# Opening of a two-layer transformer kernel: value projection on x times the norm weight, deviation applied later, ones multiplied on TensorE in the waits

## The chip, the core and the metric

The kernel runs on one core of a Trainium2 chip. The metric is the device time of one execution in microseconds (us), as the median of several runs. The core has a matrix engine (TensorE, PE in the rows; its weight loads are PEld), a vector engine (VectorE, DVE), an activation engine (ScalarE, ACT), GpSimd (POOL, almost unused here) and SyncE (SP), which issues all of the transfers of this kernel from one queue. All numbers of the kernel are float32; before a projection, the activations and the weights are each split into a rounded part (hi) and a rest (lo), and each product is taken as three matmuls, hi by hi, hi by lo and lo by hi.

## What is computed

A gated mixing block, then two transformer layers (differential attention and latent attention, each with a gated convolution feed-forward part), for 256 tokens of width 1024. The change lies in the first microseconds of the first block alone:

```
h = rmsnorm(x, norm_mix_g)            # x / sqrt(mean(x*x) + eps) * g, row by row
proj = h @ w_in                       # 1024 x 7168; split into u, v, bg, cg, xs, ga, gb
u = gelu(u)
v = rmsnorm(gelu(v), norm_v_g)
a = spatial_gating(u, v, w_s, b_s)    # u * (masked w_s @ v + b_s), 8 groups
c = bg * causal_dwconv(cg * xs, conv_w)
m = sigmoid(ga) * (a @ w_proj_a) + sigmoid(gb) * (c @ w_proj_b)
x = x + m @ w_out
...
```

The deviation of a row of x is one factor for the whole row, so v before its gelu is ((x * g) @ w_v) times that factor, and the factor can be applied to the product.

## The kernel before, in words

The program writes the order of each engine out by hand, with semaphores between the engines. Weights come in chunks n = 0, 1, 2, ...: a transfer into a landing buffer (raw, and for chunks 2 and 3 raw_start), ACT writes the hi part into a ring of four slots (whl), DVE the lo part, PE multiplies, and a chunk's slot is free once PE has used it (chunk_used). Chunks 0 to 3 (N_V) are the value projection; each is half of the 1024 rows of the weight by 512 columns. They come in two transfers each (half_landed, rest_landed) and are split in two halves (split_hi_half on ACT, line 1243; split_lo_half on DVE, line 1769), which count half_lo and lo_ready. Chunks 4 to 19 (N_MIX) are four passes over the columns of cg, xs, bg and u; they are loaded by load_mix (line 477 for the first two, line 443 after that), which waits until the landing buffer is free (lo_ready), and split as a whole (lines 1221 and 1707).

The opening, by engine:

- SP issues x_rows[0] (line 459), the identity matrix (460), norm_mix_g (461), x_rows[1] (462), and then the eight half chunks (467, 468).
- DVE sets constants (1786 to 1791), among them the zeros of wsT (1790). const_set counts them.
- PE turns norm_mix_g into columns (684), and DVE copies it to mix_g (1793). PE transposes x_rows of the first 128 tokens (turn_x, line 690) for the residual.
- ACT squares and sums the rows of x as they land (1275) and takes the root (1277); DVE takes the reciprocal (1796) and scales the rows into vtok (1797). PE transposes the scaled rows of both token blocks, and then x_rows of the second block.
- ACT rounds the transposed rows times mix_g to hT (round_h, 1248), DVE writes the rest (rest_h, 1775), with the two halves of chunk 0 among them. h_ready counts the finished tiles.
- PE's v_rows (710 to 725) multiplies chunk by chunk: stationary a tile of hT, moving 512 columns of the weight; 2 token blocks x 4 k-tiles x 3 matmuls a chunk (lines 616 to 618), 96 in all. ACT applies gelu (take_v, 1294) into vtok.
- The mixer then calls project (609 to 611) for chunks 4, 5, 6, 7. Ahead of chunk 5 PE turns the small vectors (turn_vectors), ahead of chunk 6 the rows of w_s (turn_ws, line 744), and ahead of chunk 7 it runs the spatial mixing (mix_tokens, line 766, 32 matmuls), which waits for v_norm, for ws_read (DVE's four copies in take_ws, lines 1827 and 1828) and for vec_read.
- DVE copies the transposed x out of PSUM to xT (1808); it is needed in the first block's end.

## Time and profile before

| | before |
|---|---|
| median of 3 runs | 1051.89 us (1051.37 to 1051.95) |
| the profiled execution, its own time | 1052.46 us |
| its span | 1050.7 us |
| PE busy | 1028.6 us |
| DVE busy | 729.9 us |
| ACT busy | 572.0 us |
| mean DMA rate over the span | 170 GB/s |

The page gives busy time by engine over the whole span, and the chain of work that ended last. For a change in the opening the timeline and the windows of the first 60 us are the views to read: a stretch of the timeline lists instructions in order of time, one line for a merged group, with its start, its duration, its engine and source line, what it writes and reads, its count, and in brackets the engine's idle time just before it and what ended it.

### The profile page before, as it was taken

What the parts mean: (1) busy time and instruction counts of PE and PEld (TensorE: products, weight loads), DVE (VectorE), ACT (ScalarE), POOL (GpSimd) and SP (SyncE); (2) the same over time, 40 slices, a digit from 0 to 9 for tenths busy, and PEclk for the clock granted to TensorE, in tenths of its full rate; (3) what the DMA queues carried; (4) which work ended last, traced back from release to release, by engine and by line L of the source; (5) the groups of instructions that cost most, each with busy time, mean ns of one, the idle gap of its engine ahead of it and who ended that gap; (6) DMA issues with size and microseconds to landing.
All of it is one profiled execution on the core that took longest, in us unless ns stands there. A gap on an engine that the chain in (4) does not pass through costs nothing.

```text
span 1050.7 us, 19999 instructions
## 1 busy us (share of the span) xinstructions
PE 1028.6 (98%) x7892; PEld 990.1 (94%) x7892; DVE 729.9 (69%) x969; ACT 572.0 (54%) x795; POOL 6.6 (1%) x20
## 2 busy tenths in 40 slices
PE   7999999999999999999999999999999989999997
PEld 6999999999999999978899999999989989999996
DVE  6676654558665456777878777777876577777775
ACT  6555566545443443567866555554637464555554
POOL 0000000000000000000000000000020000000000
PEclk9999999999999999999999999999999999999999
DMA  8636565455655644453555666663434374666651
GB/s 292 205 124 197 180 200 196 160 182 179 214 187 196 203 160 166 158 198 121 168 153 159 203 180 180 180 180 111 136 71 120 113 212 139 190 189 189 188 159 75
DMA packets 191266, 178.89 MB, mean 170 GB/s; under 512 B 17444, under 2 KB 169586, under 8 KB 191218
## 3 DMA queue, kind: packets, MB, share of 16 engines
q1 hardware_dynamic: 191218, 178.22, 54.6%
q8 instruction: 34, 0.56, 0.2%
q14 instruction: 14, 0.11, 0.0%
HBM read 177.15 MB, written 1.05 MB: 170 GB/s over the span
## 4 chain that ended last, share of the span: by engine, by line
PE 89%; DVE 5%; ACT 3%; DMA 2%; issue 1%; SPq 0%; DVEq 0%; ACTq 0%
PE psum L609 24%; PE psum L611 24%; PE psum L610 24%; PE psum L616 4%; PE psum L617 4%; PE psum L618 4%; DVE whl L1707 2%; ACT whl L1221 1%; PE psum L950 1%; PE psum L934 1%; PE psum L949 1%; ACT prob L1462 1%; DMA x_rows<-x 1%; DMA raw<-da_w_qkv 0%; DVE stat L2084 0%
## 5 line engine op out<-in xcount | busy, mean ns | idle before, releaser
L609 PE MATMUL psum<-hT,whl 128*128 128x256 f32 x1392 | 395.9, 284 | 4.3 <-DVE hT L1782 4.3
L611 PE MATMUL psum<-hT,whl 128*128 128x256 f32 x1392 | 394.4, 283 | 0.0
L610 PE MATMUL psum<-hT,whl 128*128 128x256 f32 x1392 | 394.3, 283 | 0.0
L1707 DVE TENSOR_TENSOR whl<-raw,whl 128x2048 fp32r<-128x2048 f32 (+2 forms) x145 | 298.3, 2063 | 92.1 <-ACT whl L1221 91.8
L1221 ACT ACTIVATE whl<-raw 128x2048 fp32r<-128x2048 f32 (+2 forms) x145 | 248.7, 1717 | 113.0 <-DMA raw<-w_ff 67.9
L609 PEld LDWEIGHTS psum<-hT,whl 128*128 128x128 f32 x1392 | 267.3, 192 | 6.0 <-DVE hT L1782 4.2
L610 PEld LDWEIGHTS psum<-hT,whl 128*128 128x128 f32 x1392 | 267.3, 192 | 0.9
L611 PEld LDWEIGHTS psum<-hT,whl 128*128 128x128 f32 x1392 | 267.3, 192 | 0.0
L609 PE MATMUL psum<-lat,whl 128*128 128x256 f32 (+1 forms) x512 | 145.8, 285 | 0.0
L610 PE MATMUL psum<-lat,whl 128*128 128x256 f32 (+1 forms) x512 | 144.7, 283 | 0.0
L611 PE MATMUL psum<-lat,whl 128*128 128x256 f32 (+1 forms) x512 | 144.7, 283 | 0.0
L1393 ACT ACTIVATE conv_out<-conv_in,vcol 128x256 f32<-128x256 f32 x88 | 48.2, 595 | 122.7 <-DVE conv_in L1983 122.7
L609 PEld LDWEIGHTS psum<-lat,whl 128*128 128x128 f32 (+1 forms) x512 | 97.2, 190 | 0.4 <-DVE k_sb L2243 0.3
L610 PEld LDWEIGHTS psum<-lat,whl 128*128 128x128 f32 (+1 forms) x512 | 97.2, 190 | 0.1
L611 PEld LDWEIGHTS psum<-lat,whl 128*128 128x128 f32 (+1 forms) x512 | 97.2, 190 | 0.0
L1981 DVE SCALAR_TENSOR_TENSOR conv_out<-conv_in,vcol,conv_out 128x256 f32<-128x256 f32 x176 | 73.6, 481 | 8.9 <-ACT conv_out L1393 8.1
L1707 DVE TENSOR_TENSOR whl<-q_sb,whl 128x2048 fp32r<-128x2048 f32 (+1 forms) x44 | 77.1, 1751 | 1.6 <-ACT whl L1221 1.6
L1983 DVE TENSOR_TENSOR conv_in<-psum,rstd 128x512 f32<-128x512 f32 x44 | 30.4, 691 | 53.2 <-PE psum L611 53.1
L1221 ACT ACTIVATE whl<-q_sb 128x2048 fp32r<-128x2048 f32 (+1 forms) x44 | 65.0, 1478 | 2.5 <-PE psum L611 2.5
L609 PE MATMUL psum<-mT,whl 128*128 128x256 f32 x192 | 54.7, 285 | 0.8 <-DVE mT L2121 0.8
L610 PE MATMUL psum<-mT,whl 128*128 128x256 f32 x192 | 53.9, 281 | 0.0
L611 PE MATMUL psum<-mT,whl 128*128 128x256 f32 x192 | 53.9, 281 | 0.0
(246 smaller groups left out, 1386.7 us busy)
## 6 DMA issues: line engine op xcount, KB each, us to landing
raw<-w_ff SPq DMA_DIRECT2D x32, 1024.0 KB, 5.5
raw<-w_in SPq DMA_DIRECT2D x24, 1024.0 KB, 5.2
raw<-ffn_w_up SPq DMA_DIRECT2D x44, 512.0 KB, 5.0
q_sb<-ffn_w_up SPq DMA_DIRECT2D x44, 512.0 KB, 5.0
raw<-da_w_qkv SPq DMA_DIRECT2D x12, 1024.0 KB, 5.2
q_sb<-ffn_w_down SPq DMA_DIRECT2D x22, 512.0 KB, 3.6
raw<-ffn_w_down SPq DMA_DIRECT2D x22, 512.0 KB, 3.6
raw<-w_proj_a SPq DMA_DIRECT2D x4, 1024.0 KB, 5.2
```

The costliest lines, as they stand in the source:

```text
L609: mm(dst, weight(n, 0, cols, kt, c0, m), hi, start=start, stop=False, skip_group_check=True)
L610: mm(dst, weight(n, 0, cols, kt, c0, m), lo, start=False, stop=False, skip_group_check=True)
L611: return mm(dst, weight(n, 1, cols, kt, c0, m), hi, start=False, stop=stop, skip_group_check=True)
L616: mm(dst, hi, w_hi, start=start, stop=False, skip_group_check=True)
L617: mm(dst, hi, w_lo, start=False, stop=False, skip_group_check=True)
L618: return mm(dst, lo, w_hi, start=False, stop=stop, skip_group_check=True)
L934: last = nc.tensor.transpose(pxs[:, c, s * P:(s + 1) * P], weights[:, c, s * P:(s + 1) * P], ident)
L1221: fn(whl[:, slot, 0, 0:w], landing(n)[:, 0:w], ACT.Copy).then_inc(hi_ready, 1)
L1393: ins = fn(conv_out[:, q, b, :], conv_in[:, q, b, 2:], ACT.Identity, bias=conv(3, b, j), scale=conv(2, b, j))
L1707: tt(whl[:, slot, 1, 0:w], landing(n)[:, 0:w], whl[:, slot, 0, 0:w].bitcast(F32), ALU.subtract).then_inc(lo_ready, 1)
L1981: return stt(dst, conv_in[:, q, b, t:SEQ + t], vcol[:, bass.ds(j + (conv_col(l - 1, t) + FB * b), 1)], dst, ALU.mult, ALU.add)
L1983: tt(conv_in[:, q, :, 2:], up[q][:], scale, ALU.mult).then_inc(f["up_read"], 1)
```

## The change

In the opening, the value projection no longer reads the normalised rows. It reads u = x times norm_mix_g, in transposed tiles of 128 x 128, held in the buffers lat (k-tiles 0 to 3) and mT (k-tiles 4 to 7), which are otherwise used later (opening, round_u, rest_u). The reciprocal deviation of the row is given to the gelu as its scale (take_v). The sums of squares, the root, the scaling of the rows (now in place in x_rows) and their transposes move behind: ACT does them after the splits of chunks 0 to 2, DVE after those splits too, and PE transposes the scaled rows between the chunks 2 and 3 of the value projection (turn_rows_of_h). round_h and rest_h, which now serve the chunks from 4 on alone, come after the gelu of the first half of v and around the splits of chunks 4 and 5; project for chunk 4 waits for their tiles one by one.

PE multiplies a 128 x 128 matrix of equal numbers by itself (busy) 10 times at the very start, 12 times between the two blocks of transposes of x, and 8 times after them. All of x is transposed before the value projection. Chunk 0 is taken in another order: k-tiles 0 and 1 of both token blocks, then 2 and 3 of both.

On SP's queue, x_rows[1] goes behind the first half of chunk 0, and the transfer of b_s waits until PE has used chunks 0 to 3. The zeros of wsT move from DVE's start to take_ws.

The diff, cut to its edits:

```diff
--- before.py
+++ after.py
@@ -342,6 +342,7 @@
...
         x_turned, x_read = sem("x_turned"), sem("x_read")
+        u_hi_ready, u_ready = sem("u_hi_ready"), sem("u_ready")
         vec_turned, vec_read = sem("vec_turned"), sem("vec_read")
...
@@ -387,6 +388,11 @@
...
+        def opening(kt):
+            return (lat if kt < KT // 2 else mT)[:, kt, :, :]
...
@@ -459,12 +465,13 @@
...
             sp.dma_start(vec_rows[0:KT, 0, :], a["norm_mix_g"].rearrange("l (r c) -> (l r) c", c=P)).then_inc(mix_landed, 16)
-            sp.dma_start(x_rows[:, 1, :], x_in[:, 1, :]).then_inc(x_landed[1], 16)
             for n in range(N_MIX):
...
                 sp.dma_start(dst[:, 0:KT // 4, :], src[:, 0:KT // 4, :]).then_inc(half_landed[n], 16)
+                if n == 0:
+                    sp.dma_start(x_rows[:, 1, :], x_in[:, 1, :]).then_inc(x_landed[1], 16)
                 sp.dma_start(dst[:, KT // 4:, :], src[:, KT // 4:, :]).then_inc(rest_landed[n], 16)
...
@@ -502,6 +509,8 @@
...
+            sp.wait_ge(chunk_used, N_MIX)
             sp.dma_start(bsb[:], a["b_s"].broadcast_to([P, A_GROUPS, P])).then_inc(bsb_landed, 16)
...
@@ -654,10 +663,6 @@
...
-            def h_tile(k):
-                return lambda kt: pe.wait_ge(h_ready, KT * k + kt + 1)
...
@@ -679,28 +684,47 @@
...
+            def busy(count):
+                for _ in range(count):
+                    mm(bank[2][:, 0, 0:P], ones[D][:], ones[D][:], start=True, stop=True)
+            pe.wait_ge(const_set, 2)
+            busy(10)
             pe.wait_ge(ident_landed, 16)
...
-            def turn_x(dst, src, t, done):
+            pe.wait_ge(mix_g_read, 1)
+            for t in range(TT):
+                if t > 0:
+                    busy(12)
+                pe.wait_ge(x_landed[t], 16)
                 for kt in range(KT):
-                    last = nc.tensor.transpose(dst[kt // 2][:, kt % 2, t * P:(t + 1) * P],
-                                               src[:, t, kt * P:(kt + 1) * P], ident)
-                    if done is not None and kt % 2 == 1:
-                        last.then_inc(done, 1)
-            pe.wait_ge(x_landed[0], 16)
-            turn_x(x_bank, x_rows, 0, None)
-            pe.wait_ge(mix_g_read, 1)
-            pe.wait_ge(xn_ready, 1)
-            turn_x(bank, vtok, 0, None)
-            pe.wait_ge(xn_ready, 2)
-            turn_x(bank, vtok, 1, xn_turned)
-            pe.wait_ge(x_landed[1], 16)
-            turn_x(x_bank, x_rows, 1, x_turned)
+                    last = nc.tensor.transpose(x_bank[2 * t + kt // 4][:, kt % 4 // 2, kt % 2 * P:(kt % 2 + 1) * P],
+                                               x_rows[:, t, kt * P:(kt + 1) * P], ident)
+                    if kt % 4 == 3:
+                        last.then_inc(x_turned, 1)
+            busy(8)
+            def turn_rows_of_h():
+                pe.wait_ge(x_read, 4)
+                for t in range(TT):
+                    pe.wait_ge(xn_ready, t + 1)
+                    for kt in range(KT):
+                        last = nc.tensor.transpose(x_bank[kt // 2][:, kt % 2, t * P:(t + 1) * P],
+                                                   x_rows[:, t, kt * P:(kt + 1) * P], ident)
+                        if t == TT - 1 and kt % 2 == 1:
+                            last.then_inc(xn_turned, 1)
+            def h_tile(k):
+                return lambda kt: pe.wait_ge(h_ready, KT * k + kt + 1)
...
@@ -710,22 +734,27 @@
                 order = [(t, at) for t in range(TT) for at in range(KT // 2)]
+                if n == 0:
+                    order.sort(key=lambda o: o[1] // 2)
                 for t, at in order:
...
                         pe.wait_ge(lo_ready, n + 1)
-                    if t == 0 and n < 2:
-                        pe.wait_ge(h_ready, max(2, kt + 1))
+                    if n < 2:
+                        pe.wait_ge(u_ready, KT * t + kt + 1)
                     w_hi, w_lo = [weight(n, part, 2 * PAIR, at, 0, 2 * PAIR) for part in range(2)]
-                    last = tokens(flat(bank[n // 2 * 2 + t]), n, w_hi, w_lo, hi_lo(hT, kt), t, kt == 0, kt == KT - 1)
+                    last = tokens(flat(bank[n // 2 * 2 + t]), n, w_hi, w_lo, (opening(kt)[:, 0, :], opening(kt)[:, 1, :]), t, kt == 0,
+                                  kt == KT - 1)
                     if t == 0 and kt == KT - 1:
...
                 v_rows(N_V + c)
+                if c == 2:
+                    turn_rows_of_h()
...
@@ -754,7 +783,8 @@
...
                         mix_tokens()
-                    project(N_MIX + s, hT, i)
+                    first = s == 0 and spatial
+                    project(N_MIX + s, hT, i, first=h_tile(MIX) if first else None)
...
@@ -877,7 +907,6 @@
...
-            pe.wait_ge(const_set, 2)
             pe.wait_ge(const_landed, 16)
...
@@ -1242,10 +1271,17 @@
...
+            def round_u(t, kts):
+                for kt in kts:
+                    act.wait_ge(x_turned, 2 * t + kt // 4 + 1)
+                    fn(opening(kt)[:, 0, t * P:(t + 1) * P], x_bank[2 * t + kt // 4][:, kt % 4 // 2, kt % 2 * P:(kt % 2 + 1) * P],
+                       ACT.Identity, scale=mix_g[:, kt:kt + 1]).then_inc(u_hi_ready, 1)
...
                 act.wait_ge(xn_turned, kt // 2 + 1)
-                fn(hT[:, kt, 0, :], bank[kt // 2][:, kt % 2, :], ACT.Identity, scale=mix_g[:, kt:kt + 1]).then_inc(h_hi, 1)
+                fn(hT[:, kt, 0, :], x_bank[kt // 2][:, kt % 2, :], ACT.Identity, scale=mix_g[:, kt:kt + 1]).then_inc(h_hi, 1)
...
@@ -1265,25 +1301,29 @@
...
+            x_bank = [up[0], up[1], px, py]
+            half = KT // 2
             act.wait_ge(const_set, 1)
-            fn(eps[:, 1:2], eps[:, 0:1], ACT.Sqrt)
+            fn(eps[:, 1:2], eps[:, 0:1], ACT.Identity)
+            act.wait_ge(mix_g_read, 1)
+            round_u(0, range(0, half))
+            split_hi_half(0, 0)
+            round_u(0, range(half, KT))
+            round_u(1, range(0, half))
+            split_hi_half(0, 1)
+            round_u(1, range(half, KT))
+            for n in (1, 2):
+                split_hi_half(n, 0)
+                split_hi_half(n, 1)
             x_flat = t_act[:].rearrange("p a b c -> p (a b c)")
             for t in range(TT):
-                act.wait_ge(x_landed[t], 16)
                 if t > 0:
...
                 fn(x_flat, x_rows[:, t, :], ACT.Square, accum_out=xstat[:, 0, t:t + 1]).then_inc(x_sq, 1)
-                act.wait_ge(x_sq, t + 1)
-                fn(xstat[:, 1, t:t + 1], xstat[:, 0, t:t + 1], ACT.Sqrt, bias=eps[:, 0:1], scale=1.0 / D).then_inc(x_std, 1)
-            split_hi_half(0, 0)
-            act.wait_ge(mix_g_read, 1)
-            for kt in range(KT):
-                if kt == KT // 2:
-                    split_hi_half(0, 1)
-                round_h(kt)
-            split_hi_half(1, 0)
-            split_hi_half(1, 1)
+            act.wait_ge(x_sq, TT)
+            fn(xstat[:, 1, :], xstat[:, 0, :], ACT.Sqrt, bias=eps[:, 0:1], scale=1.0 / D).then_inc(x_std, 1)
+            split_hi_half(3, 0)
+            split_hi_half(3, 1)
...
@@ -1292,18 +1332,15 @@
...
                 fn(vtok[:, t, 2 * g * PAIR:2 * (g + 1) * PAIR], bank[2 * g + t][:].rearrange("p a b -> p (a b)"),
-                   ACT.Gelu).then_inc(bank_free[2 * g + t], 1)
-            for c in range(4):
-                n = N_V + c
-                if n + LEAD < N_MIX:
-                    split_hi_half(n + LEAD, 0)
-                    split_hi_half(n + LEAD, 1)
-                else:
-                    split_hi(n + LEAD)
-                if c == 1:
-                    for t in range(TT):
-                        take_v(0, t)
+                   ACT.Gelu, scale=xstat[:, 2, t:t + 1]).then_inc(bank_free[2 * g + t], 1)
+            act.wait_ge(xn_ready, 1)
+            take_v(0, 0)
+            take_v(0, 1)
+            split_hi(N_MIX)
+            for kt in range(KT):
+                round_h(kt)
+            split_hi(N_MIX + 1)
             t_flat = t_act[:].rearrange("p a b c -> p (a b c)")
...
@@ -1772,7 +1809,7 @@
...
                 dve.wait_ge(h_hi, kt // 2 * 2 + 2)
-                stt(hT[:, kt, 1, :], bank[kt // 2][:, kt % 2, :], mix_g[:, kt:kt + 1], hT[:, kt, 0, :].bitcast(F32),
+                stt(hT[:, kt, 1, :], x_bank[kt // 2][:, kt % 2, :], mix_g[:, kt:kt + 1], hT[:, kt, 0, :].bitcast(F32),
                     ALU.mult, ALU.subtract).then_inc(h_ready, 1)
...
@@ -1787,25 +1824,42 @@
...
                 nc.vector.memset(ones[w][:], 1.0 / w)
-            nc.vector.memset(wsT[CHUNK:P, :, 0:CHUNK], 0.0)
             nc.vector.memset(conv_in[:, :, :, 0:2], 0.0).then_inc(const_set, 1)
...
             copy(mix_g[:], bank[3][:, 0, 0:KT]).then_inc(mix_g_read, 1)
-            for t in range(TT):
-                dve.wait_ge(x_std, t + 1)
-                step.wait(step.mark(nc.vector.reciprocal(xstat[:, 2, t:t + 1], xstat[:, 1, t:t + 1])))
-                ts(vtok[:, t, :], x_rows[:, t, :], xstat[:, 2, t:t + 1], None, ALU.mult).then_inc(xn_ready, 1)
+            x_bank = [up[0], up[1], px, py]
+            def rest_u(t, kts):
+                for kt in kts:
+                    dve.wait_ge(u_hi_ready, KT * t + kt // 4 * 4 + 4)
+                    stt(opening(kt)[:, 1, t * P:(t + 1) * P], x_bank[2 * t + kt // 4][:, kt % 4 // 2, kt % 2 * P:(kt % 2 + 1) * P],
+                        mix_g[:, kt:kt + 1], opening(kt)[:, 0, t * P:(t + 1) * P].bitcast(F32), ALU.mult,
+                        ALU.subtract).then_inc(u_ready, 1)
+            half = KT // 2
+            dve.wait_ge(mix_g_read, 1)
+            rest_u(0, range(0, half))
             split_lo_half(0, 0)
-            dve.wait_ge(mix_g_read, 1)
-            for kt in range(KT):
-                if kt == KT // 2:
-                    split_lo_half(0, 1)
-                rest_h(kt)
+            rest_u(0, range(half, KT))
+            rest_u(1, range(0, half))
+            split_lo_half(0, 1)
+            rest_u(1, range(half, KT))
             split_lo_half(1, 0)
             split_lo_half(1, 1)
-            for b, src in enumerate((up[0], up[1], px, py)):
-                dve.wait_ge(x_turned, b + 1)
-                copy(xT[:, 2 * b:2 * b + 2, :], src[:]).then_inc(x_read, 1)
+            for t in range(TT):
+                for b in range(2):
+                    copy(xT[:, 4 * b:4 * b + 4, t * P:(t + 1) * P],
+                         x_bank[2 * t + b].rearrange("p a (b c) -> p (a b) c", c=P)).then_inc(x_read, 1)
+            split_lo_half(2, 0)
+            split_lo_half(2, 1)
+            dve.wait_ge(x_std, 1)
+            step.wait(step.mark(nc.vector.reciprocal(xstat[:, 2, :], xstat[:, 1, :])))
+            dve.wait_ge(x_turned, 4)
+            for t in range(TT):
+                ts(x_rows[:, t, :], x_rows[:, t, :], xstat[:, 2, t:t + 1], None, ALU.mult).then_inc(xn_ready, 1)
+            split_lo_half(3, 0)
+            split_lo_half(3, 1)
...
@@ -1821,6 +1875,7 @@
...
+                nc.vector.memset(wsT[CHUNK:P, :, 0:CHUNK], 0.0)
                 for u in range(2):
...
@@ -1839,13 +1894,10 @@
...
-            for c in range(4):
-                n = N_V + c + LEAD
-                if n < N_MIX:
-                    split_lo_half(n, 0)
-                    split_lo_half(n, 1)
-                else:
-                    split_lo(n)
+            split_lo(N_MIX)
+            for kt in range(KT):
+                rest_h(kt)
+            split_lo(N_MIX + 1)
             dve.wait_ge(v_std, 1)
...
             for t in range(TT):
```

## Rows read from the trace of the kernel before

**Rows 1.** The page, part 1 and part 4: busy engines, and the chain.

```profile
PE 1028.6 (98%) x7892; PEld 990.1 (94%) x7892; DVE 729.9 (69%) x969; ACT 572.0 (54%) x795; POOL 6.6 (1%) x20
...
PE 89%; DVE 5%; ACT 3%; DMA 2%; issue 1%; SPq 0%; DVEq 0%; ACTq 0%
```

**Rows 2.** Busy time by stretch, core's first 50 us; header line names the columns.

```profile
core 0: us, PE busy (x) PEld busy (x) DVE busy (x) ACT busy (x) POOL busy (x), PEclk, DMA share, GB/s
0.00:10.00 10.00, 4.08 (x17) 3.31 (x17) 2.91 (x12) 5.18 (x9) 0.20 (x4) 1.00 0.77 265
10.00:20.00 10.00, 9.77 (x43) 8.69 (x44) 9.42 (x16) 9.12 (x16) 0.00 (x0) 1.00 1.03 370
...
40.00:50.00 10.00, 10.00 (x88) 10.00 (x87) 8.62 (x14) 4.21 (x4) 0.00 (x0) 1.00 0.55 181
```

**Rows 3.** Timeline of PE, first 14.6 us and where chunk 4 begins.

```profile
4.56 0.24 PE L684 MATMUL psum<-const,vec_rows 8*128 8x8 f32 x1 [4.56 <-DMA vec_rows<-norm_mix_g]
4.73 1.97 PE L690 MATMUL psum<-const,x_rows 128*128 128x128 f32 x8
6.76 1.94 PE L690 MATMUL psum<-const,vtok 128*128 128x128 f32 x8
10.23 1.97 PE L690 MATMUL psum<-const,vtok 128*128 128x128 f32 x8 [1.53 <-DVE vtok L1797]
11.99 1.92 PE L690 MATMUL psum<-const,x_rows 128*128 128x128 f32 x8
13.56 0.67 PE L616 MATMUL psum<-whl,hT 128*128 128x512 f32 x1
...
14.07 0.40 PE L617 MATMUL psum<-whl,hT 128*128 128x512 f32 x1
...
14.30 0.40 PE L618 MATMUL psum<-whl,hT 128*128 128x512 f32 x1
...
35.65 0.28 PE L609 MATMUL psum<-hT,whl 128*128 128x256 f32 x1
```

**Rows 4.** The chain in order of time, later small matmuls: start, duration, line, count.

```profile
47.75 0.88 PE psum L744 x8
...
54.38 3.57 PE psum L766 x32
```

**Rows 5.** Timeline of DVE and ACT, first 24 us.

```profile
1.50 0.48 DVE L1790 MEMSET wsT<- 64x512 f32 x1
4.83 0.17 DVE L1793 COPY mix_g<-psum 128x8 f32<-128x8 f32 x1 [2.74 <-PE psum L684]
7.72 1.06 ACT L1275 ACTIVATE t_act<-x_rows 128x1024 f32<-128x1024 f32 x1 [2.09 <-DMA x_rows<-x]
9.42 0.75 DVE L1797 TENSOR_SCALAR vtok<-x_rows,xstat 128x1024 f32<-128x1024 f32 x1
16.74 3.95 ACT L1243 ACTIVATE whl<-raw_start 128x1024 fp32r<-128x1024 f32 x4
18.55 2.48 DVE L1808 COPY xT<-psum 128x512 f32<-128x512 f32 x4
20.71 1.28 ACT L1294 ACT_TABLE_LOAD   x1
20.94 4.62 DVE L1769 TENSOR_TENSOR whl<-raw_start,whl 128x1024 fp32r<-128x1024 f32 x4
```

**Rows 6.** Transfers: first half of chunk 0 (issued 2.46), then its rest (2.93).

```profile
raw<-w_in SPq DMA_DIRECT2D x1, 512.0 KB, 6.5
...
raw<-w_in SPq DMA_DIRECT2D x1, 512.0 KB, 7.4
```

**Rows 7.** Groups by line and shape: busy, mean ns of one, idle before.

```profile
L1486 ACT ACTIVATE t_act<-hf 128x128 f32<-128x128 f32 x16 | 4.7, 302 | 0.9 <-DVE hf L2108 0.9
L1775 DVE SCALAR_TENSOR_TENSOR hT<-psum,mix_g,hT 128x256 fp32r<-128x256 f32 x8 | 3.3, 476 | 0.6 <-ACT hT L1248 0.6
```

**Rows 8.** Timeline of DVE and ACT, 25 to 54 us, and PEld at mix_tokens.

```profile
39.32 0.17 DVE L1850 RECIPROCAL vstat<-vstat 128x2 f32<-128x2 f32 x1 [7.42 <-ACT vstat L1316]
...
47.79 0.69 DVE L1887 TENSOR_TENSOR conv_in<-psum,t_act 128x512 f32<-128x512 f32 x1 [0.36 <-PE psum L611]
...
49.30 1.92 ACT L1221 ACTIVATE whl<-raw 128x2048 fp32r<-128x2048 f32 x1 [5.29 <-DMA raw<-w_in]
...
53.27 0.43 DVE L1828 COPY wsT<-psum 64x256 f32<-64x256 f32 x1
...
54.10 3.66 PEld L766 LDWEIGHTS psum<-wsT,vtok 128*128 128x128 f32 x32
54.22 3.73 PE L766 MATMUL psum<-wsT,vtok 128*128 128x128 f32 x32
```

## The prediction

> **What bounds the kernel now.** I began with the page: TensorE is busy 1028.6 of 1050.7 us, and 89% of the chain that ended last is its own [rows 1]. Then the windows of the opening: in the first 10 us TensorE works 4.08 us, in the next ten 9.77, later all of it [rows 2]. So the idle time that a change of the opening can give back lies before 10.2 us. Then TensorE's timeline: it waits for the transfers until 4.56, works through the first transposes, waits 1.53 us (1.9 with its weight loads) for the scaled rows of the second token block, and runs without a gap from 10.23 [rows 3]. The chain behind that wait is plain in the other engines' rows: x_rows[1] lands at 7.7, is squared, scaled from 9.42 on, transposed [rows 5]. Last, the spacing of instructions shows a second loss. Eight transposes take 1.97 us with the 0.42 us of the last one's own duration in it, so one comes every 0.22 us [rows 3]; eight of the same kind at 47.75 take 0.88, 0.11 each [rows 4]. The granted clock reads 1.00 in all windows [rows 2] and does not show it, but the spacing is that of 1.2 GHz early and of 2.4 GHz late. The first matmul of 512 columns starts at 13.56, the second at 14.07 (0.51 us, low clock), the third at 14.30 (0.23, high clock) [rows 3]: the clock rose at about 14.
>
> From 13.56 the 96 matmuls of the value projection take 96 x 0.227 = 21.8 us plus 0.28 for the first, and chunk 4 starts at 35.65 [rows 3]. From there TensorE is never idle for long, so the whole is a matter of when the work behind the opening begins. I sum everything as a shift of that start, and add it to the end.
>
> **The change part by part.** *TensorE's work.* It transposes 32 tiles before and 32 after; what moves is that the 16 of the scaled rows now stand between chunks 2 and 3 at the high clock, on the path: 16 x 0.11 = 1.76 us [rows 4]. If the value projection begins at S, chunk 4 begins at S + 21.8 + 1.8 = S + 23.5, a shift of S - 12.1 against 35.65. The change gains only if S is below 12.1.
>
> *The ones.* A product of 128 x 128 by 128 columns costs 3.57 / 32 = 0.11 us at the high clock [rows 4] and 0.22 at the low one, as the transposes do [rows 3]. Ten from about 1.6 (the zeros of wsT, 0.48 us [rows 5], no longer stand before the count they wait for) end at 3.8, before the row of norm_mix_g is there at 4.56: free. TensorE now waits for the copy of mix_g, which ends at 5.00 [rows 5], so the first block of x is transposed from 5.05 instead of 4.73 to 6.8. Twelve ones: to 9.5 at the low clock.
>
> *x_rows[1] behind the first half of chunk 0.* Before, the one landed at 7.7 [rows 5], the other at 2.46 + 6.5 = 9.0, the rest of chunk 0 at 10.3 [rows 6]. Both are 512 KB, so I let them change places: the weights at 7.8, x at 9.0; bounds for x 8.3 and 10.3. It is thus about there when the twelve ones end.
>
> *Clock.* All low: transposes 9.5 to 11.3, eight ones to 13.0, so S = 13.0. All high from 8.9 on: x is awaited to 9.0, transposes to 9.9, ones to 10.8, S = 10.8. Before, the clock rose after 3.8 us of unbroken work from 10.23; but the 4 us from 4.56, with a gap of 0.4 us in the weight loads, didn't raise it [rows 3]. After, the work is unbroken from 5.05 while x is in time, so I expect the rise between 8.9 and 12.4; at 10.3, the middle, S = 11.6. That is my value.
>
> The Trainium skill speaks against this in "TensorE: Matmul & The Clock Gate", Part 4: transposes are said not to count as work that lets the clock rise. By that rule only the ones would count, and it is the first rival below. In this trace 16 transposes and half a microsecond of matmuls stood before the rise, which speaks against the rule.
>
> *ACT and DVE.* They must deliver as fast. A rounding of a 128 x 128 tile on ACT takes 302 ns by the nearest row, a rest on DVE less than the 476 ns of a 128 x 256 one [rows 7]; back to back I take 0.27 and 0.26. ACT: first four tiles 6.2 to 7.3, first half of chunk 0 7.8 to 8.8, four tiles to 9.9, four of the second block (transposed by 10.5) to 11.6, second half of chunk 0 to 12.6. DVE follows: first half's lo at 10.2, below S; second half's lo at 13.9. TensorE wants it at S + 12 x 0.227 = 14.3, since chunk 0 now begins with tiles 0 and 1 of both blocks. No stall at S = 11.6; at S = 10.8 one of up to 0.4. Chunk 1 is ready at 17.5 (wanted 18.4). The copies to xT, 2.48 us, and the halves of chunk 2 at 1.15 each [rows 5] end at 22.3 (wanted 23.9). Squares, a table load of 1.28 [rows 5], and root end on ACT at 22, the scaled rows on DVE at 23.6; TensorE wants them at 27.9. Chunk 4's lo is there at 30.2 and the last tile of h at 33.5, for a start at 35.1. The margins are over one microsecond, so these parts cost nothing; if they all came 1.6 us later, the excess would go to the path.
>
> *Queues.* load_mix of chunk 7 waits for chunk 5's lo, now about 36.7, and lands at about 42.6; chunk 7 is wanted at 54. The wait before b_s stands behind it in the queue, ends at 35, and b_s is read at 57. ACT waits 5.29 us for chunk 8 as it is [rows 8]. Free.
>
> *The zeros of wsT.* 0.48 us plus a gap, 0.52, now stand in DVE's row from 47.79, which waits for TensorE (0.36 us idle) and therefore moves with it, to the last copy of take_ws, over at 53.70. TensorE's weight load at 54.10 waits for that copy [rows 8]: slack 0.34 with the signal, so 0.52 costs 0.18 us, on the path.
>
> *Sum:* 11.6 - 12.1 + 0.18 = -0.35 us. Bounds: S = 10.8 with its stall -0.8, all high and the zeros hidden -1.3; S = 13.0 gives +1.1. The profiled execution took 1052.46 with a span of 1050.7; it would take 1052.1. It stands 0.6 above the median of 1051.89, which the same shift brings to 1051.5.
>
> **The rivals.** *The clock stays low until the projection has run for a while (slower).* Place: twelve and eight ones with eight transposes between them, if transposes and the small matmuls don't suffice, or a wait for x breaks the work. S = 13.0, and the matmuls of chunk 0 pay 0.2 us each until the rise: at 14 the total is +1.1 + 0.4 + 0.2 = +1.6, 1053.5, still in the band of no change; if the rise waits for 3.8 us of projection, to 17, ten matmuls pay and the stalls of chunk 0 lie under them: +2.9, 1054.8. It becomes slower than 0.2% from a rise at about 15. For it: 4 us of transposes at 4.56 didn't raise the clock. Against: the 3.8 us from 10.23 did.
>
> *x lands late.* Behind four transfers instead of three; if it comes at 12 the transposes end at 13 to 14, ACT's rounding of the second block holds chunk 0 and the total is about +2.5, 1054.4. Against: the landings before are 1.3 us apart [rows 6].
>
> *The chain is shorter than I take it.* If the first half of chunk 0 lands at 7.0, x at 8.0 and the clock is high by then, S is 9.8 and the lo of the second half comes at 12.4: -2.3 + 0.2, 1049.8. It needs three things at once.
>
> *The change does nothing it says:* the ones neither raise the clock nor does S move below 12.1; that is the first rival's milder half.
>
> **How the numbers follow.** About 0.2%, 2.1 us, is what a measurement of this kernel can tell from no change. My forecast, S from 10.8 to 12.7, 1050.6 to 1052.7: 0.72. Low clock till 14, 1053.5: 0.12. Low clock till 17, 1054.8: 0.05. Late x, 1054.4: 0.04. Shorter chain, 1049.8: 0.07. So faster 0.07, same 0.84, slower 0.09. The range leaves out the last three in the main and reaches from 1050.2 to 1053.6.
>
> **What would show it.** In the profile after: first transposes at 5.05; x_rows[1] landed at 9.0; the spacing of the eight transposes of block two and of the ones after them, 0.22 turning to 0.11; first matmul of 512 columns at 11.6; 16 transposes at about 28 that take 1.8 us; project of chunk 4 from 35.1 without a wait for h_ready; a short wait of TensorE for wsT's last copy at 54. Wrong if the first matmul of 512 columns starts below 10 or above 14, or if chunk 4 waits for DVE.

## The result, and the profile after

| | before | changed |
|---|---|---|
| median | 1051.92 us (6 runs, 1051.33 to 1053.64) | 1056.07 us (6 runs, 1054.13 to 1056.97) |
| ratio to before, 95% interval | | 1.0036 (1.0024 to 1.0048) |
| the profiled execution, its own time | 1052.46 us | 1056.26 us |
| its span | 1050.7 us | 1054.5 us |

The change makes the kernel slower by 4.1 us between the medians, 0.36% by the ratio. The forecast was 1051.5, no change, with a range to 1053.6; the result lies outside it.

The page of the changed kernel, parts 1 and 4, answers to [rows 1]:

```profile
PE 1034.7 (98%) x7952; PEld 996.2 (94%) x7952; DVE 734.0 (70%) x984; ACT 577.2 (55%) x811; POOL 6.6 (1%) x20
...
PE 89%; DVE 5%; ACT 3%; DMA 1%; issue 1%; DVEq 0%; ACTq 0%
```

TensorE executes 60 matmuls more. The program has 30 products of ones. So each product is two matmuls, which the prediction had not counted. TensorE's timeline of the changed kernel, the opening, answers to [rows 3]:

```profile
1.42 4.64 PE L691 MATMUL psum<-ones 128*128 128x128 f32 x20 [1.42 <-DVE conv_in L1827]
5.98 0.27 PE L697 MATMUL psum<-const,vec_rows 8*128 8x8 f32 x1
6.51 1.54 PE L707 MATMUL psum<-const,x_rows 128*128 128x128 f32 x8 [0.26 <-DVE mix_g L1829]
7.89 2.84 PE L691 MATMUL psum<-ones 128*128 128x128 f32 x24
10.57 1.04 PE L707 MATMUL psum<-const,x_rows 128*128 128x128 f32 x8
11.45 1.95 PE L691 MATMUL psum<-ones 128*128 128x128 f32 x16
13.15 0.48 PE L625 MATMUL psum<-whl,lat 128*128 128x512 f32 x1
...
37.10 0.28 PE L618 MATMUL psum<-hT,whl 128*128 128x256 f32 x1
```

The chain of work that ended last (start, duration, line, count) runs in the same execution, from 1.42 to 13.4 us, through the ones and the transposes:

```profile
1.42 4.64 PE psum L691 x20
6.51 1.54 PE psum L707 x8
8.05 2.68 PE psum L691 x24
10.74 0.87 PE psum L707 x8
11.61 1.79 PE psum L691 x16
```

The first row of ones lasts to 6.0, past the 4.56 at which norm_mix_g had been there [rows 3]. The clock rises in the first transposes of x (eight in 1.54 us, then eight in 1.04), some 6 us earlier than in the kernel before. What follows at the high clock is mostly the multiplying of ones: 2.68 and 1.79 us in the chain. The value projection starts at 13.15, against 13.56, and chunk 4 at 37.10, against 35.65: a shift of 1.45 us.

The shift grows twice more. I set the n-th matmul of one trace, counted from the end, against the n-th of the other. The shift is 1.45 us at chunk 4, 2.1 to 2.2 from the spatial mixing on, 2.0 up to 507 us, and 3.8 from 513 to the end. The timeline of ACT, DVE and TensorE up to the spatial mixing, changed kernel, answers to [rows 8]:

```profile
44.05 1.92 ACT L1250 ACTIVATE whl<-raw 128x2048 fp32r<-128x2048 f32 x1 [0.39 <-DMA raw<-w_in]
...
46.00 2.29 DVE L1744 TENSOR_TENSOR whl<-raw,whl 128x2048 fp32r<-128x2048 f32 x1 [0.75 <-ACT whl L1250]
...
49.71 0.69 DVE L1939 TENSOR_TENSOR conv_in<-psum,t_act 128x512 f32<-128x512 f32 x1 [0.32 <-issue]
...
53.43 0.48 DVE L1878 MEMSET wsT<- 64x512 f32 x1 [0.17 <-DVE conv_out L1928]
...
55.81 0.43 DVE L1883 COPY wsT<-psum 64x256 f32<-64x256 f32 x1
...
56.34 3.81 PE L796 MATMUL psum<-wsT,vtok 128*128 128x128 f32 x32 [0.51 <-issue]
```

TensorE waits 0.51 us for the last copy of take_ws, which ends at 56.24; the view calls it "issue", since it names no releaser. The second growth is at the load of the attention's output weight. The waits of 495 to 516 us (who waited for whom, total, times, longest) in the kernel before:

```profile
ACT whl L1221 <- DMA raw<-da_w_o: 1.2, 1, 1.2
```

and in the changed kernel:

```profile
ACT whl L1250 <- DMA raw<-da_w_o: 2.9, 1, 2.9
...
PE psum L978 <- ACT k_sb L1568: 1.2, 1, 1.2
```

### The profile page after: what moved, and what is told of

It is laid out like the page before. It is cut to its first block, busy times and chain, and to the rows that moved or that the text cites. A ratio compares the mean times of both kernels' runs of the same rounds, so it can differ in the third digit from the quotient of the medians.

```text
span 1054.5 us, 20151 instructions
## 1 busy us (share of the span) xinstructions
PE 1034.7 (98%) x7952; PEld 996.2 (94%) x7952; DVE 734.0 (70%) x984; ACT 577.2 (55%) x811; POOL 6.6 (1%) x20
## 4 chain that ended last, share of the span: by engine, by line
PE 89%; DVE 5%; ACT 3%; DMA 1%; issue 1%; DVEq 0%; ACTq 0%
PE psum L618 24%; PE psum L619 24%; PE psum L620 24%; PE psum L625 4%; PE psum L626 4%; PE psum L627 4%; DVE whl L1744 2%; ACT whl L1250 1%; PE psum L691 1%; PE psum L979 1%; DMA raw<-da_w_o 1%; PE psum L963 1%; PE psum L978 1%; ACT prob L1499 1%; DVE stat L2136 0%
## 5 line engine op out<-in xcount | busy, mean ns | idle before, releaser
L2035 DVE TENSOR_TENSOR conv_in<-psum,rstd 128x512 f32<-128x512 f32 x44 | 30.4, 691 | 53.2 <-PE psum L620 53.1
```

The source lines that it names most:

```text
L2035: tt(conv_in[:, q, :, 2:], up[q][:], scale, ALU.mult).then_inc(f["up_read"], 1)
```

## The experiments

Each time is a median beside the median of the kernel before measured with it, which lies between 1051.9 and 1052.2. Where one is set against the changed kernel, it is against 1056.07.

**Half of the ones.** `busy(5)`, `busy(6)`, `busy(4)` for 10, 12, 8:

```diff
-            busy(10)
+            busy(5)
-                    busy(12)
+                    busy(6)
-            busy(8)
+            busy(4)
```

> The changed kernel with 5, 6 and 4 products of ones instead of 10, 12 and 8; nothing else. Theory (a product of ones is two weight loads and two matmuls, so it costs 0.43 us at the low and 0.22 us at the high clock, twice what the prediction took): the first row of ones is over at 3.6 instead of 6.1, norm_mix_g is turned at 4.56 instead of 5.98, the value projection starts between 10.8 and 12.5 instead of 13.15, most likely 11.7, and the kernel is 1.4 us faster than the changed one, about 1054.6 against 1056.1. Rival (the loss comes from elsewhere, the ones only fill waits): the value projection starts within 0.3 us of 13.15 and the time is within 0.5 us of the changed kernel's. Second rival (fewer ones, later rise of the clock): the start is early but matmuls of 512 columns take 0.43 us each until 14, and half of the gain is gone.

Measured: 1053.40 us against 1051.90, ratio 1.0009 (1.0001 to 1.0018), so 2.7 us less than the changed kernel. TensorE's timeline of the opening:

```profile
1.42 2.50 PE L691 MATMUL psum<-ones 128*128 128x128 f32 x10 [1.42 <-DVE conv_in L1827]
4.58 0.24 PE L697 MATMUL psum<-const,vec_rows 8*128 8x8 f32 x1 [0.66 <-DMA vec_rows<-norm_mix_g]
5.08 1.97 PE L707 MATMUL psum<-const,x_rows 128*128 128x128 f32 x8 [0.26 <-DVE mix_g L1829]
6.84 2.77 PE L691 MATMUL psum<-ones 128*128 128x128 f32 x12
9.40 1.92 PE L707 MATMUL psum<-const,x_rows 128*128 128x128 f32 x8
11.11 1.10 PE L691 MATMUL psum<-ones 128*128 128x128 f32 x8
11.97 0.48 PE L625 MATMUL psum<-whl,lat 128*128 128x512 f32 x1
```

This is the opening that the prediction described, line by line: transposes from 5.08 (5.05), ones to 9.4 (9.5), the clock's rise in the last row of ones, the projection at 11.97 (11.6). The double price of the ones is shown. Chunk 4 starts at 35.9, a shift of 0.25, so 1.2 us earlier than in the changed kernel, and the mixing 1.7 us earlier. The median fell by 2.7, twice the 1.4 that were expected; the opening does not account for all of it, and the profiled execution, at 1056.26 us, was the slowest of the twelve.

**No ones.** All three calls of busy taken out.

> The changed kernel without any product of ones. Theory (the ones cost more on the path than the higher clock gives back): transposes from 5.05 at 0.22 us each, x_rows[1] awaited to 8.9, value projection from 10.7 at the low clock, 0.43 us a matmul, until the clock rises; if it rises at 14, chunk 4 starts 0.8 us earlier than in the changed kernel, about 1055.3; if it rises at 12, 1.8 us earlier, 1054.3. Rival (the clock is what the opening lives on): the clock rises only at 17 or later and the kernel is slower than the changed one, 1057 or more.

Measured: 1052.93 us against 1051.90, ratio 1.0008 (0.9999 to 1.0017). TensorE's timeline:

```profile
5.02 1.97 PE L704 MATMUL psum<-const,x_rows 128*128 128x128 f32 x8 [0.26 <-DVE mix_g L1825]
9.38 1.97 PE L704 MATMUL psum<-const,x_rows 128*128 128x128 f32 x8 [2.38 <-DMA x_rows<-x]
11.00 0.78 PE L625 MATMUL psum<-whl,lat 128*128 128x512 f32 x1
11.57 0.63 PE L626 MATMUL psum<-whl,lat 128*128 128x512 f32 x1
12.00 0.63 PE L627 MATMUL psum<-whl,lat 128*128 128x512 f32 x1
```

The first matmuls of 512 columns come at the low clock, one every 0.43 us (the first takes 0.57), and the clock rises at about 14. The kernel still is 3.1 us faster than the changed one. So the clock is worth something: each of six matmuls cost 0.20 us more, 1.2 us in all. The 30 products spent more than that. Chunk 4 starts at 36.27, 0.8 us earlier than in the changed kernel, just as expected for a rise at 14. The time, however, is 2.4 us below the 1055.3 expected with it, so here too the median fell by more than the opening shows.

**u in another buffer.** k-tiles 4 to 7 of u in a buffer at hf's address; in return the zeros of wsT are set on DVE at the start, and b_s is loaded without its wait.

```diff
-            return (lat if kt < KT // 2 else mT)[:, kt, :, :]
+            if kt < KT // 2:
+                return lat[:, kt, :, :]
+            return u_more[:, kt - KT // 2, :, :]
...
-            sp.wait_ge(chunk_used, N_MIX)
...
-                nc.vector.memset(wsT[CHUNK:P, :, 0:CHUNK], 0.0)
```

> The changed kernel with k-tiles 4 to 7 of u in a buffer at hf's address instead of mT; since mT lies over wsT and bsb, the zeros of wsT can then be set on DVE at the start again and b_s loaded without the wait for chunk 3; both are done here. Theory 1 (the zeros in take_ws hold the spatial mixing): TensorE's wait of 0.51 us ahead of mix_tokens is gone and the kernel is 0.5 us faster than the changed one. Theory 2 (matmuls whose stationary tile is read from mT's address are slower, 0.233 against 0.227 us): with hf they take 0.227, another 0.3 us, 1055.3 in all. Rival for 2 (the spacing belongs to chunks 1 and 3, not to the buffer): 0.233 stays, gain 0.5 us at most.

Measured: 1054.36 us against 1051.90, ratio 1.0026 (1.0016 to 1.0037), 1.7 us less than the changed kernel. Three rows of TensorE's timeline of the changed kernel, chunk 3, whose stationary tiles come from mT:

```profile
35.24 0.40 PE L626 MATMUL psum<-whl,mT 128*128 128x512 f32 x1
35.47 0.39 PE L627 MATMUL psum<-whl,mT 128*128 128x512 f32 x1
35.70 0.40 PE L625 MATMUL psum<-whl,mT 128*128 128x512 f32 x1
```

There the mean spacing is 0.2333 us in chunks 1 and 3, in each of five profiles that read mT, against 0.2267 in chunk 2, which reads lat. With the other buffer chunk 1 is back at 0.2267 and chunk 3 at 0.2285, with its slower ones right behind the transposes. So 48 matmuls cost 48 x 0.0066 = 0.3 us through the buffer alone. What a buffer's address has to do with the spacing is not shown. At the mixing, DVE's last copy ends at 54.88 and TensorE starts without a wait:

```profile
55.40 1.83 PE L800 MATMUL psum<-wsT,vtok 128*128 128x128 f32 x15
```

The distance from chunk 4 to the mixing is 18.57 us, that of the kernel before, instead of 19.24. In the trace both theories hold: chunk 4 comes 0.26 us and the mixing 0.94 us earlier than in the changed kernel. The median fell by 1.7 us instead of the 0.8 expected, but 1 us lies within what two series of these kernels can differ by, as the kernel before once more shows below.

**The changed kernel once more.**

> The changed kernel unchanged, as a second profile. In the first one the shift against the kernel before is 1.45 us where chunk 4 starts, 2.13 after the spatial mixing, and 3.79 at the end; 1.6 us came in between 507 and 516, where the transfer of da_w_o landed late. Theory (the 1.6 us are chance of that execution and its transfers): this profile has the first two shifts within 0.3 us, and the wait at 508 differs, by up to 2 us in either direction, so the time of single executions spreads by that much. Rival (the shifted opening makes the later transfer late): the wait for da_w_o is 2.9 us again and the end is shifted by 3.8 again.

Measured: 1055.93 us against 1051.90, ratio 1.0037 (1.0025 to 1.0050). In this profile the clock was high from 5.9 us, before the first transposes of x (eight in 1.09 us), the projection started at 12.64, and chunk 4 was shifted by 0.9 us, the mixing by 1.5. So the opening itself spreads by half a microsecond from one execution to the next, and the expected 0.3 us were too few. ACT's wait for da_w_o was 1.9 us: less than 2.9, more than the 1.2 of the kernel before. The end is shifted by 2.0 us, not 3.8, so the rival does not hold as put, but the late transfer is there again.

**Small products in the kernel before.** 8 products of 8 x 8 ahead of the wait for the identity, 7 between the transposes of the scaled blocks.

```diff
+            def small(count):
+                for _ in range(count):
+                    mm(px[0:8, 1, P:P + 8], ones[D][:, 0:8], ones[D][:, 0:8], start=True, stop=True)
...
+            small(8)
...
             turn_x(bank, vtok, 0, None)
+            small(7)
```

> The kernel before with 15 products of 8 x 8 on TensorE in its idle time (8 ahead of the wait for the identity, 7 between the transposes of the two scaled blocks): as many instructions, 60, as the ones of ones_half, and nothing on the path. Theory (the instructions added shift the blocks in which TensorE's instructions are fetched; in the kernels with ones a fetch falls at 500 to 502 us, into the transfer of da_w_o, which then lands late, in the two profiles without ones it falls at 508 to 509): the fetch is at about 500 here too, TensorE or ACT wait 0.5 to 2 us longer around 508, and the time is 0.7 to 1.5 us above the kernel before although the opening is the same within 0.2 us. Rival (chance): same time as the kernel before within 0.4 us. The clock may rise earlier through the small products, worth up to 1.5 us the other way; the trace shows it.

Measured: 1051.84 us against 1052.23, ratio 0.9998 (0.9989 to 1.0006). The 16 KB fetch moved from 508 to 498 us as expected, and nothing came of it: ACT waited 1.1 us. The theory as put fell. What remained was that the 8 KB fetch had stayed at 506.3.

The opening wasn't the same, though. In this profile the clock rose at 10.4 us instead of 13 to 14, and it brought little:

```profile
8.74 0.51 PE L684 MATMUL psum<-ones 128*8 128x8 f32 x14
9.18 1.65 PE L696 MATMUL psum<-const,vtok 128*128 128x128 f32 x8
10.67 1.04 PE L696 MATMUL psum<-const,x_rows 128*128 128x128 f32 x8
11.95 0.47 PE L616 MATMUL psum<-whl,hT 128*128 128x512 f32 x1 [0.24 <-DVE hT L1782]
```

TensorE now waits for hT, and later for the second half of chunk 0. Chunk 4 starts at 34.3, 0.2 us before it does in the two profiles below that have this opening without the small products.

**The zeros of wsT alone, in the kernel before.** The memset of line 1790 moved into take_ws.

> The kernel before with the zeros of wsT set in take_ws, as the change does, and nothing else. Theory (DVE's row up to the last copy of take_ws holds mix_tokens): the copy ends at 54.2 instead of 53.7, the 32 small matmuls begin 0.2 to 0.6 us later and the whole is 0.2 to 0.6 us longer, 1052.3. The prediction took 0.18, the changed kernel showed 0.67 between chunk 4 and the mixing. Rival: it costs nothing, same as before within 0.1 in the trace at 54 us.

Measured: 1052.25 us against 1052.23. In the trace, the mixing starts 18.77 us after chunk 4 instead of 18.57, so 0.20 us are lost. That is the prediction's 0.18, and below what the total time tells.

**The kernel before once more.**

> The kernel before, unchanged, as a second profile. The opening should agree within 0.3 us, up to the point where the clock rises (theory: the rise isn't tied to the program, so the first matmul of 512 columns may come at either clock); the fetch of instructions near 508 us should recur within 1 us and ACT's wait for da_w_o should be 0.9 to 1.5 us. Rival (chance in the transfers): a wait for da_w_o of 2 us or more in this profile too.

Measured: 1051.20 us against 1052.23. TensorE's timeline:

```profile
8.97 1.97 PE L690 MATMUL psum<-const,vtok 128*128 128x128 f32 x8 [0.36 <-DVE vtok L1797]
10.73 1.92 PE L690 MATMUL psum<-const,x_rows 128*128 128x128 f32 x8
12.30 0.78 PE L616 MATMUL psum<-whl,hT 128*128 128x512 f32 x1
```

The opening did not agree within 0.3 us. x_rows[1] landed at 6.4 us instead of 7.7, so the second block of scaled rows came 1.3 us earlier than in [rows 3], and chunk 4 at 34.5 instead of 35.65. In before_small and before_zeros, whose openings are nearly the same, x_rows[1] landed at 6.2 and 6.6 and chunk 4 starts at 34.3 and 34.6. The one profile that the prediction rested on was the latest of four, by 1.1 us. The fetches (506.6 and 507.1 us) and ACT's wait (1.3 us) were as expected.

The time says something too. This is the same kernel as the one beside it, and its median of nine executions lies 1.0 us lower (ratio 0.9993, 0.9984 to 1.0002). So a difference of 1 us between two medians of this document can be chance.

**Other buffer and six ones.** u_in_hf with `busy(6)` between the blocks of transposes, and no other ones.

> The changed kernel with u's k-tiles 4 to 7 at hf's address (and zeros and b_s as in the kernel before), and of the ones only 6 products, between the two blocks of transposes. Theory (what remains of the change when the ones are priced rightly and the buffer is another): norm_mix_g turned at 4.55, transposes from 5.05 to 6.8, ones to 9.4, transposes to 11.1, value projection from 11.0, with some matmuls at 0.43 us until the clock rises between 10 and 13; chunk 4 starts between 35.0 and 35.9, mixing within 0.5 us of the kernel before; 24 instructions more than before. Time 1051.5, if the fetch of instructions doesn't fall into da_w_o's transfer; 1052.5 if it does.

Measured: 1050.82 us against 1052.23, ratio 0.9991 (0.9982 to 1.0000). The opening came earlier than expected: the clock rose at 8.7, not after 10, the projection started at 9.80 and chunk 4 at 34.1, below the 35.0 to 35.9 that were expected. **The same again:**

> hf_0_6_0 unchanged, once more, against the kernel before. Theory (its opening is worth about 0.6 us, chunk 4 at 34.2 to 35 against 34.3 to 35.7, and no pair of fetches meets da_w_o's transfer): median 0.5 to 1.5 us below the kernel before's, ratio 0.9990. Rival (the first measurement was luck): within 0.3 us of the kernel before.

Measured: 1050.82 us against 1052.09, ratio 0.9992 (0.9984 to 1.0001). The two medians lie 1.4 and 1.3 us below those of the kernel before. Each interval reaches 1, and the kernel before once more lay 1.0 us below itself, so a small gain is likely and not shown. In the traces chunk 4 starts at 34.1 and 33.9, 0.2 to 0.7 us before the three profiles above. TensorE's timeline of the second:

```profile
4.93 1.97 PE L710 MATMUL psum<-const,x_rows 128*128 128x128 f32 x8 [0.26 <-DVE mix_g L1832]
6.69 2.31 PE L695 MATMUL psum<-ones 128*128 128x128 f32 x12
8.84 1.04 PE L710 MATMUL psum<-const,x_rows 128*128 128x128 f32 x8
9.71 0.49 PE L629 MATMUL psum<-whl,lat 128*128 128x512 f32 x1
```

x_rows[1] landed at 8.1 us and the ones end 0.7 us later. The clock rose among them, and the projection starts at 9.71 at the high clock. At 12.96 TensorE waits 0.23 us for the second half of chunk 0, so an earlier start would have gained little. Why the clock rose at 8.4 and 8.7 here, and at 11.2 in ones_half with the same six products in this gap and five more ahead of them, is open.

**Five, twelve, eight.** The changed kernel with the first row of ones halved.

> The changed kernel with 5 products of ones at the start instead of 10. Theory (the first row's second half, past 4.56, is pure loss): norm_mix_g is turned at 4.57 instead of 5.98 and the value projection starts 1.4 us earlier than the changed kernel's if the clock rises as early, about 11.9, with the second row costing 5.1 at the low clock or 2.7 at the high one. Median 1055 against 1056, between the changed kernel and ones_half. Rival (the first row is what raises the clock at 6 to 8 us; with 5 it rises at 10 or later): the second row then takes 4 us or more, and the value projection starts at 13 or later, no gain against the changed kernel.

Measured: 1056.60 us against 1052.09, ratio 1.0038 (1.0023 to 1.0053): no gain.

```profile
6.73 4.05 PE L691 MATMUL psum<-ones 128*128 128x128 f32 x24
```

The rival forecast the times rightly: the second row (24 matmuls) took 4.05 us, not 2.84, and the projection started at 13.20. The clock rose at 9.3 instead of 7.5. That the shorter first row is what delayed it is not shown, since in hf_again, with no first row at all, it rose at 8.4. Here the load of chunk 7 landed at 44.9 (44.0 in the changed kernel), DVE waited 1.58 us for ACT's part of it (0.75), and TensorE 1.3 us at the mixing.

**Both fetches together, the opening good.** hf_0_6_0 with 9 small products in the first idle time.

> hf_0_6_0 with 9 products of 8 x 8 in TensorE's idle time before the identity lands: 60 instructions more than the kernel before instead of 24, opening otherwise the same. In the profiles so far, da_w_o's transfer landed late (ACT waited 1.9 to 3.5 us, TensorE 0.2 to 1.8 us for k_sb) in those four where two fetches of instructions, of 16 KB and of 8 KB, both began within 0.4 us of 500 us (counted in the kernel before's time), and on time (0.9 to 1.3 us) in the six where only one did or none. Theory (the pair delays it): here the 16 KB one moves to the 8 KB one, ACT waits 2 us or more, and the median is 0.7 to 1.5 us above hf_0_6_0's 1050.8. Rival (the late landing is chance or belongs to something else of the change): median within 0.4 us of 1050.8, wait about 1.

Measured: 1051.32 us against 1052.09, ratio 0.9996 (0.9987 to 1.0005), 0.5 us above hf_0_6_0. The queues of instructions between 498 and 500.5 us in this kernel (packets, MB, share) show that both fetches fell there:

```profile
q8 instruction: 1, 0.02, 2.6%
q14 instruction: 1, 0.01, 1.1%
```

In hf_again the same question for 496 to 500 us gives one of them, and the other follows at 503:

```profile
q14 instruction: 1, 0.01, 0.8%
```

ACT waited 1.6 us (1.0 in hf_0_6_0 and hf_again). The expected wait of 2 us or more and the 0.7 us in the median were not reached. The wait points the way of the theory, but is shorter than in any of the profiles that it was made from; 0.5 us in the median can be chance.

## Why the prediction was wrong, point by point

**The ones: the step that failed.** The prediction read 3.57 us for x32 at line 766 [rows 4] and took 32 for the number of products. The code issues 8 groups by 2 blocks there, 16 products. Each float32 product is two matmuls with two weight loads (20 in the first row's line for ten calls), unlike a transpose, which is one (8 for eight). A product of ones costs 0.22 us at the high and 0.43 at the low clock. So the ten took 4.64 us and not 2.2, put norm_mix_g off from 4.56 to 5.98, and the second and third row took 4.5 us of the chain at the high clock, where 20 products at the prediction's 0.11 come to 2.2. The projection started at 13.15 instead of 11.6. The kernel with half of them started it at 11.97, within the bounds of 10.8 and 12.7, and 1.2 us before the changed one.

This step alone would have left the result in the range: with S at 13.15 the prediction's own sum gives +1.2 us, 1053.1. The measured shift is 4.1 us against a sum of -0.35. Besides the 1.55 us of S, it took the path up to chunk 4 (0.4), the load of chunk 7 (0.5), the late profile the sum was set against (1.1) and the load at 500 us (0.8 and 1.7 in the two profiles). Halving the ones took 2.7 us of the 4.1 away and leaving them out 3.1, more than the 1.7 and 1.3 us by which the mixing came earlier in the two traces. The remainder lies behind the opening, or is chance.

**The clock.** Its rise was looked for between 8.9 and 12.4; it came at 5.9 and 7.5 in the two profiles of the changed kernel, at the end of the first row of ones and in the first transposes, and at 11.2 in ones_half, inside. The value of 10.3 was called the middle of the bounds, which is 10.65; that moves S by less than 0.2. The first rival (low clock to 14 or 17) didn't come to pass; in ones_none it rose at 14 and cost 1.2 us. The Trainium skill's rule in "TensorE: Matmul & The Clock Gate", Part 4, that transposes don't let the clock rise, isn't decided: in both profiles of the kernel before it rose after transposes and at most two projection matmuls (at 14.0 and 12.9), which speaks against it. In the kernels with ones it rose after ones, and in ones_none it rose at 13.8, after six projection matmuls, which fits it.

**The path between.** S + 23.5 was to give chunk 4. With S = 13.15 that is 36.7, and it came at 37.1. The 0.3 us of mT's slower spacing were put at nothing in the sum; the 16 transposes took 1.75 us in the chain (1.76 forecast). Right were also: x_rows[1] at 8.9 (2.51 + 6.4; 9.0 forecast), the first half of chunk 0 at 7.5 (7.8), and the margins of ACT and DVE up to chunk 4: TensorE waited for none of them.

**The zeros of wsT.** 0.18 forecast, 0.20 alone in the kernel before. But the changed kernel lost 0.67 there. "Free" was said of chunk 7, whose load now waits for a later lo of chunk 5: it was issued at 38.2 (36.7 forecast) and landed at 44.0 (42.6 forecast), ACT waited 0.39 us for it, and its split on DVE started at 46.00, after a wait of 0.75 us (0.62 before). Measured from chunk 4, that split ends 0.5 us later than in the kernel before, and it pushed the whole row of DVE up to take_ws. I had looked at when TensorE wants chunk 7 (54 us) and not at what stands behind its split on DVE. Nor had I seen why the zeros move at all: mT lies over wsT and bsb, so the choice of buffer forces both the memset and the wait of b_s.

**The load at 500 us** stood in no rival. The changed kernel's median lies 4.1 us above; its opening explains about 2.6, the distance of the means at the mixing (56.3 and 55.7, against 54.2, 53.1, 52.9 and 53.3 in the four profiles with the opening of before). Of the rest, 1.5 us, its two profiles show 1.7 and 0.8 coming in between 507 and 513. There ACT waited for da_w_o 1.9 to 3.5 us in five profiles, and 0.9 to 1.6 in the other eight. The 3.5 us are those of ones_half's slowest execution. In those five, and in hf_small with 1.6, a 16 KB and an 8 KB fetch of instructions began within 0.5 us of each other near 500 us, while that transfer was under way. In the seven others at most one of them fell there; in the kernel before both come at 508, when the chunk has landed at 504.6. So instructions added at the start move fetches that come hundreds of microseconds later. That the pair causes the late landing is not shown. It fits all thirteen profiles, but hf_small made the pair and ACT waited only 0.6 us longer than in hf_again, and whether something else of the changed opening takes part stays open.

**The anchor.** The shift was summed against one profile whose chunk 4 stood at 35.65, where three others have 34.3 to 34.6. Against those the changed opening is 2.0 to 2.8 us late at chunk 4, not 1.45, and a forecast with S = 11.6 would have given +0.8 us rather than -0.35.

**The spread.** A stretch of 15 us around 857 us shows one reason why single executions differ by one or two microseconds whatever the opening. TensorE has been idle for 3.34 us there, in the kernel before up to 856.41:

```profile
856.41 0.39 PE L609 MATMUL psum<-hT,whl 128*128 128x256 f32 x1 [3.34 <-DVE hT L1782]
```

The gap is the same in every profile, but what the clock does after it isn't: it was low for 3.4 us in ten of the thirteen profiles, for 6.8 in two, and not at all in u_in_hf. The granted clock (the column after POOL) in the kernel before, in ones_half and in u_in_hf:

```profile
850.00:865.00 15.00, 11.66 (x83) 11.28 (x82) 12.42 (x15) 11.52 (x15) 0.00 (x0) 0.89 0.73 206
```

```profile
850.00:865.00 15.00, 11.66 (x74) 11.21 (x73) 11.92 (x13) 10.06 (x13) 0.00 (x0) 0.77 0.75 207
```

```profile
850.00:865.00 15.00, 11.66 (x93) 11.24 (x93) 11.91 (x13) 10.07 (x13) 0.00 (x0) 1.00 0.75 208
```

Against the kernel before, ones_half lost 0.9 us in it and u_in_hf gained 1.4. A comparison of two profiled ends says little here; the shift at a named instruction says more.

## What to carry to other kernels

Before an instruction is priced by a row, divide the row's count by the number of calls in the code: a float32 product is two matmuls here, a transpose one. Filler work belongs only where it ends before what TensorE waits for is there. In the changed kernel the first row ended 1.4 us after norm_mix_g could have been turned, and the second 1.7 us after x_rows[1] had landed. The kernel with six products in one gap had the high clock when its projection began, as the one with thirty did, and began it 3.4 us earlier. Measure by how much two series of the same kernel differ before giving a difference of that size a cause. When a buffer is borrowed, look up what else lies at its address, since that decides which work and which loads have to move with it, and follow a moved load to what is queued behind its split.

## What the runs showed of the hardware that I had not expected

- A matmul of 512 columns whose stationary tile is read from mT's address came every 0.2333 us (five profiles), from lat's, hT's or hf's every 0.2267 us.
- The same program did not get the high clock at the same place: the changed kernel, with its first matmul at 1.42 us both times, at 7.5 us in one profile and at 5.9 in the other.
- With 15 products of 8 x 8 in the gaps, 1.1 us of TensorE's time, the clock rose at 10.4 us (one profile), and at 12.9 to 14.0 in three without them.
- With 24 to 120 more instructions on TensorE in the first 13 us a 16 KB fetch of instructions came at 498 to 503 us, and without them at 507 to 509.
